# Expert gather with the down and the up row in one transfer, each row weighed by ScalarE as it comes

## The reference

```python
# q: 8 heads; two top-16 searches over 128 keys, and a top 16 over their 256 sums
eidx = ...                       # [T, 8 * 16]: 128 experts for each token
gate = softmax(top_s)            # [T, 8, 16]
def one(hh, ee, gg):             # 128 tokens at once
    a = einsum("tkd,td->tk", peer_down[ee], hh)   # 128 rows of 1024 for each token
    act = gg * gelu(a)
    return einsum("tk,tkd->td", act, peer_up[ee])
```

## Time and profile before

| | us |
|---|---|
| time, median of 3 runs (4175.64 to 4180.74) | 4179.28 |
| span of the profiled execution (the page gives no time outside it) | 4362.9 |
| TensorE busy | 3358.4 |
| VectorE busy | 2577.2 |
| ScalarE busy | 816.5 |
| GpSimd busy | 2040.9 |

### The profile page before, as it was taken

How to read it: one execution, slowest core, us unless ns; L and a number is a source line. 1 busy time by engine, 2 the same in 40 slices (tenths; PEclk the granted TensorE clock), 3 DMA queues, 4 the chain that set the end, 5 groups by cost and what they waited for, 6 DMA issues and landing times.

```text
span 4362.9 us, 35889 instructions
## 1 busy us (share of the span) xinstructions
PE 3358.4 (77%) x11238; PEld 1715.0 (39%) x11238; DVE 2577.2 (59%) x5454; ACT 816.5 (19%) x1926; POOL 2040.9 (47%) x2148
## 2 busy tenths in 40 slices
PE   6889686888767787887687766766878887866766
PEld 2357442356434243551354422221366654422111
DVE  1412768566686846676357674666563347684776
ACT  1311111321211122121211111111231211111111
POOL 0210566655555666666116665566000005676665
PEclk9999899999979899996899988866988998999556
DMA  6663998999999999999849999999400039999999
GB/s 228 227 237 130 338 363 320 375 356 409 401 362 355 343 378 352 392 410 375 298 159 369 333 365 392 372 405 374 157 1 1 1 113 338 352 350 372 379 369 346
DMA packets 380787, 1330.31 MB, mean 305 GB/s; under 512 B 39500, under 2 KB 44876, under 8 KB 377016
## 3 DMA queue, kind: packets, MB, share of 16 engines
q0 software_dynamic: 313344, 1141.10, 69.3%
q1 hardware_dynamic: 61104, 164.18, 10.1%
q10 hardware_dynamic: 6152, 22.74, 1.4%
HBM read 1326.69 MB, written 1.17 MB: 304 GB/s over the span
## 4 chain that ended last, share of the span: by engine, by line
PE 15%; DVE 10%; DMA 9%; issue 7%; POOL 5%; another core or an unknown queue 3%; ACT 2%; ACTq 0%; DVEq 0%; POOLq 0%
PE ps L1701 15%; POOL arena L3075 5%; DMA arena<-in_peer_up,arena 5%; DVE arena L893 3%; DVE arena L906 3%; DMA arena<-in_peer_v,arena 2%; ACT arena L2462 1%; DMA arena<-in_ada_w 1%; DMA arena<-in_peer_u,arena 1%; DMA arena<-in_peer_down,arena 1%; PE ps L1707 1%; DVE arena L914 1%; DVE arena L1287 1%; DVE arena L1282 0%
## 5 line engine op out<-in xcount | busy, mean ns | idle before, releaser
L1701 PE MATMUL ps<-arena 128*128 128x512 f32 (+9 forms) x10500 | 3254.6, 490 | 873.9 <-ACT arena L2462 231.9
L1701 PEld LDWEIGHTS ps<-arena 128*128 128x128 f32 (+4 forms) x10500 | 1621.6, 196 | 2435.2 <-issue 1844.2
L906 DVE SCALAR_TENSOR_TENSOR arena<-arena,ps 128x1024 f32<-128x1024 f32 x1024 | 1240.6, 1217 | 542.1 <-DMA arena<-in_peer_down,arena 289.1
L3075 POOL DMA_INDIRECT arena<-in_peer_down,arena x768 | 747.1, 973 | 654.8 <-DVE arena L910 269.5
L3075 POOL DMA_INDIRECT arena<-in_peer_up,arena x768 | 736.5, 959 | 541.2 <-PE ps L1701 294.3
L2462 ACT ACTIVATE arena<-arena 128x128 f32<-128x128 f32 (+5 forms) x1242 | 444.4, 387 | 1890.8 <-PE ps L1701 636.3
L3075 POOL DMA_INDIRECT arena<-in_peer_u,arena x256 | 248.4, 970 | 647.9 <-DVE arena L910 543.6
L906 DVE SCALAR_TENSOR_TENSOR ps<-arena,ps 128x512 f32<-128x512 f32 x508 | 383.4, 755 | 143.0 <-DMA arena<-in_peer_up,arena 88.8
L2462 ACT ACTIVATE arena<-ps 128x512 f32<-128x512 f32 (+4 forms) x349 | 191.5, 549 | 1165.6 <-PE ps L1701 547.9
L3075 POOL DMA_INDIRECT arena<-in_peer_v,arena x256 | 242.4, 947 | 149.2 <-issue 59.9
L893 DVE TENSOR_TENSOR arena<-arena 128x512 f32<-128x512 f32 (+8 forms) x398 | 246.9, 620 | 72.1 <-ACT arena L2462 42.1
(11 more groups left out here) (34 smaller groups left out, 565.1 us busy)
## 6 DMA issues: line engine op xcount, KB each, us to landing
arena<-in_w_mod POOLq DMA_DIRECT2D x40, 1024.0 KB, 6.6
arena<-in_gate_blocks SPq DMA_DIRECT2D x16, 2048.0 KB, 7.8
arena<-in_w_in SPq DMA_DIRECT2D x14, 2048.0 KB, 7.9
arena<-in_w_pq SPq DMA_DIRECT2D x13, 2048.0 KB, 16.0
arena<-in_ada_w POOLq DMA_DIRECT2D x24, 1024.0 KB, 8.3
arena<-in_w_out SPq DMA_DIRECT2D x8, 2048.0 KB, 8.0
arena<-in_gate_blocks SPq DMA_DIRECT2D x8, 1792.0 KB
arena<-mod_scratch ACTq DMA_DIRECT2D x26, 512.0 KB
```

The lines of the kernel that those rows point to most:

```text
L906: self.e.scalar_tensor_tensor(o, a, s, b, op0, op1, accum_out=accum).then_inc(*(inc or self.inc(self.S.vec)))
L1701: return self.e.matmul(o, l, r, start=start, stop=stop)
L3075: self.e.indirect_dma_start(out=o, out_offset=None, in_=table, in_offset=bass.IndirectOffsetOnAxis(ap=idx.bitcast(U32), axis=0)).then_inc( ...
```

## The change

- The host lays the down and the up row of an expert side by side in one table (`peer_rows`, `peer_rows_2`; a row of 2048 floats, 8 KB). One indirect DMA a step brings both into one of NR = 6 buffers of 8 KB a partition. GpSimd waits only until row s - 6 has been used up (`freed`).
- LAG becomes 1. ScalarE weighs each row at once (`weigh`): for the tanh form Square, Copy, Tanh and Identity on one column, for the exact form Gelu and Copy, then the diagonal as before. Each of these waits for the instruction before it. The constants of the tanh form are folded into the scale of the sum on VectorE and into the gates.
- The activation in groups of 16 and its multiplication on VectorE go. In odd tiles VectorE waits for the diagonal of row s - 1 before it adds its half.
- `fold` has three instructions instead of four and no buffer of its own. Some thresholds of `weave` are written relative to LAG, so that this work starts earlier by the 17 steps.
- The arena grows by 6 KB a partition and the scratch for descriptors shrinks from 8192 to 2048 bytes.

```diff
-ND = NU = 5
-GK = 16
-LAG = GK + 2
+NR = 6
+ASK = 16
+LAG = 1
...
+    def place(self, c):
+        return self.K.rows[c % NR], (self.S.row_in[c % NR], 16 * (c // NR + 1))
...
 # VectorE, gather
-                d, there = self.down_place(s)
+                buf, there = self.place(base + s)
                 self.wait_ge(*there)
-                self.stt(d, d, 1.0, K.HP, M, M, inc=self.inc(S.down), free=True, accum=K.AA[n % 2][:, k:k + 1])
-            if s >= GK + 1 and (s - 1) % GK == 0 and s - 1 <= total:
...
-                self.tt(w[:, ks], w[:, ks], K.GT[:, tiles[n_], ks], M, inc=self.inc(S.weighted), free=True)
+                d = buf[:, 0:D]
+                self.stt(d, d, GELU_Z if l < 2 else 1.0, K.HP, M, M, inc=self.inc(S.down), free=True, accum=K.AA[n % 2][:, k:k + 1])
...
+                    src, w = buf[:, D + 512:2 * D], K.AW[n % 2][:, k:k + 1]
+                    self.wait_ge(S.diagonal, c + 1)
...
 # TensorE, gather
-                buf, there = self.up_place(u, total)
+                buf, there = self.place(c)
...
 # ScalarE, gather
-                self.act(K.AW[n_ % 2][:, ks], K.AA[n_ % 2][:, ks], gelu, inc=self.inc(S.activated))
...
+                self.wait_ge(S.down, c + 1)
+                self.weigh(l, K.AA[n % 2][:, k:k + 1], K.GT[:, tiles[n], k:k + 1], K.AW[n % 2][:, k:k + 1], c % 2)
                 if c >= 4:
                     self.wait_ge(S.up_tensor, c - 3)
-                self.act(K.dg[c % 4], K.ident, ACT.Copy, scale=K.AW[n % 2][:, k:k + 1], inc=self.inc(S.diagonal), free=True)
+                self.act(K.dg[c % 4], K.ident, ACT.Copy, scale=K.AW[n % 2][:, k:k + 1], inc=self.inc(S.diagonal))
...
+    def weigh(self, l, a, gate, w, i):
+        cube, gated, curve = (self.K.curve[:, 3 * i + j:3 * i + j + 1] for j in range(3))
+        if l < 2:
+            self.act(cube, a, ACT.Square, scale=GELU_Q)
+            self.act(gated, a, ACT.Copy, scale=gate)
+            self.act(curve, cube, ACT.Tanh, scale=a, bias=a)
+            self.act(w, curve, ACT.Identity, scale=gated, bias=gated)
+        else:
+            self.act(curve, a, ACT.Gelu)
+            self.act(w, curve, ACT.Copy, scale=gate)
...
 # GpSimd, gather
-                if s >= ND:
-                    self.wait_ge(S.down, c - ND + 1)
...
-                o, there = self.down_place(s)
-                self.fetch(o, down, K.EI[:, tiles[n], k:k + 1], there[0])
...
-                self.fetch(o, up, K.EI[:, tiles[n], k:k + 1], there[0])
+                self.freed(max(0, s - NR + 1))
+                o, there = self.place(base + s)
+                self.fetch(o, table, K.EI[:, tiles[n], k:k + 1], there[0])
```

More of the change, by code:

```diff
@@ L147, in __init__ @@
         self.rows, self.units = 0, 0
-        self.base, self.shared, self.gathers = 0, 0, 0
+        self.base, self.shared = 0, 0
         self.halves_in = 0
@@ L485, in peer_topk, with gather @@
         yield from self.peer_pick(l, t, m, 0, 8)
-    def gather(self, tiles, tables, gelu, rows):
+    def gather(self, l, tiles, rows):
         total = NEXT * len(tiles)
@@ L717, in main @@
         done = self.until(queries, (0, 0))
-        self.weave(self.gather([0, 1, 2, 3], tables, gelu, [(0, 0, 5), (0, 0, 5), (0, 1, 5), (0, 1, 5)]),
+        self.weave(self.gather(0, [0, 1, 2, 3], [(0, 0, 5), (0, 0, 5), (0, 1, 5), (0, 1, 5)]),
                    ctx_then_x(queries), RATE0, done=done)
@@ L760, in queries_then_second @@
             self.second_mu()
-            yield ("after", NEXT + 5)
+            yield ("after", NEXT + LAG - 13)
             self.second_asked()
@@ L769, in queries_then_second @@
                 yield from self.z_block(0, j)
-        self.weave(self.gather([0, 1], tables, gelu, [(1, 0, 5), (1, 0, 5)]), queries_then_second(queries), RATE1, done=done)
+        self.weave(self.gather(1, [0, 1], [(1, 0, 5), (1, 0, 5)]), queries_then_second(queries), RATE1, done=done)
         self.folded(6)
@@ L1372, in gather @@
                 c = base + u
-                w = K.AW[n % 2][:, k:k + 1]
-                buf, there = self.up_place(u, total)
                 if n % 2:
[L1376 to L1389, removed]
+                    buf, _ = self.place(c)
+                    src, w = buf[:, D + 512:2 * D], K.AW[n % 2][:, k:k + 1]
+                    self.wait_ge(S.diagonal, c + 1)
+                    if self.halves(u):
+                        self.wait_ge(S.up_vector, self.halves(u))
+                    if k == 0:
+                        self.wait_ge(S.tile_done, c // NEXT)
+                        self.ts(K.av, src, w, None, M, None, inc=self.inc(S.up_vector), free=True)
+                    else:
+                        self.stt(K.av, src, w, K.av, M, AD, inc=self.inc(S.up_vector), free=True)
+                if k == NEXT - ASK:
                     gate = self.row()
@@ L2413, in steps @@
                         i.then_inc(*self.fill(made[d]))
-            self.place()
+            self.place_out()
             yield
@@ L2441, in steps, with place_out @@
         if bt == 3:
-            self.place()
-    def place(self):
+            self.place_out()
+    def place_out(self):
         K, S = self.K, self.S
@@ L3028, in modhalf, with gather @@
         yield from self.units_of(2)
-    def gather(self, tiles, tables, gelu, rows):
+    def gather(self, l, tiles, rows):
         K, S = self.K, self.S
         base, total = self.base, NEXT * len(tiles)
-        down, up = tables
+        table = K.A["peer_rows"] if l < 2 else K.A["peer_rows_2"]
         for s in range(total + LAG):
@@ L3258, in memory @@
     K.GR = GR = here()
[L3259 removed]
+    K.BG, K.GR2 = GR + 10 * D, GR + 4096
     K.wbuf += [arena[:, GR:GR + 4096], arena[:, KCR:KCR + 4096], arena[:, K.BG + 8320:K.BG + 12416]]
     K.sums = [K.wbuf[2][:, 0:2048], K.wbuf[2][:, 2048:4096], arena[:, NB:NB + 2048]]
[L3262 to L3266 removed]
+    gm = Mem(arena, (GR, K.BG), (NB, NB + 3 * D + 6))
+    K.rows = [gm(2 * D) for _ in range(NR)]
+    K.dg, K.AA, K.AW, K.curve = [gm(128) for _ in range(4)], [gm(128) for _ in range(2)], [gm(128) for _ in range(2)], gm(6)
     K.HP, K.ap, K.av = K.psum[:, 0:1024], K.psum[:, 1024:1536], K.psum[:, 1536:2048]
```

104 lines of the change are left out of this document (27 added, 77 removed).

## The result

The changed kernel takes **4312.5 us** (4306.3 to 4327.1, four runs) beside 4180.0 us (4175.6 to 4183.0) of the kernel before: ratio 1.0324, 95% interval 1.0304 to 1.0343. It is 132 us slower; 4030 was forecast, faster.

A forecast was written before the change was run, and what follows sets the result against it. Bound: gathers whose DMA engines, ceiling near 411 GB/s, run short because GpSimd is only 3% faster. Plain -64, edges -11, woven -80 make -155: 4363 to 4208, times 0.958 gives 4030 us; own range 3950 to 4120, 8 in 10 3900 to 4215.

The forecast's parts named there:

- so I scale all: Whole kernel: the profiled forecast of 4208 us was multiplied by 0.958, timed median over profiled span, giving 4030.
- plain term of -64: Gather stretches with little or no other work woven in: 723 us become 659 at 411 GB/s.
- GpSimd, transfers: Gathers: one indirect DMA fewer a step, 1270 us less; transfers stay at 411 GB/s, 3% either way.
- stays under 2.55 a step: ScalarE gains some 1060 us of work, an estimated 1.85 us a step, yet fits the 2.55 us DMA step.
- landing term: Row buffers: a row takes 6.6 us to land, part of the 12.2 us that its buffer is held.
- slack of 3.1 us: Row buffers: six allow 15.3 us at 2.55 a step, against 12.2 us that a row is held.
- Woven stretches, -80: Gather stretches with other work woven in: faster transfers save 80 us, bounds -231 and +168.
- bound of +168: Woven stretches, slow side: a 20.5 us loop over six buffers makes 678 steps of 3.42 us, +168 us.
- I take half: Woven stretches: of about 165 us gain, half was taken, as sum, weighing and TensorE now follow one another.
- Six buffers are too few: Rival, woven stretches: copies waiting for TensorE delay weighing and buffer release, so GpSimd stops; 4269 us, chance 0.20.
- Tables: Rival, ScalarE: Tanh shares no function set with woven Exp and Sigmoid, up to 192 us of loads; 4215, chance 0.04.
- the edges, -11: Starts and ends of the gathers: 332.9 us become 322 at 411 GB/s plus landings and tails, -11 us.

The follow-up runs named there:

- a_free: The changed kernel with constant weights, so the weighing is left out and ScalarE waits for no sum; 4120.0 us.
- b_again: The kernel before, unchanged, profiled again because its first profiled execution (span 4362.9 us) was odd; 4179.1 us, profiled span 4175.9.
- b_load: The kernel before with four chained activations on a constant column ahead of every diagonal, results unused; 4295.7 us.
- a_five: The changed kernel with five buffers of 8 KB instead of six; 4407.2 us.
- a_lag3: The changed kernel with TensorE and VectorE's second half three rows behind the sum instead of one; 4416.3 us.
- a_free5: The changed kernel with constant weights, the weighing left out, and five buffers in place of six; 4205.1 us.
- v_gelu2: The changed kernel two rows behind, layers 0 and 1 weighed by two activations (Gelu's tanh form, then the gate) in place of four; 4224.1 us.

## Why the prediction was wrong

Two steps failed. The first is the slack read from the odd execution: a_free, which has all of the change but the weighing, took 4120, so 90 of the 282 us between the forecast 4030 and 4312 are gains that aren't there even without it. The second is the woven stretches: the weighing's order there was named as a cost and got no price of its own, only half of a gain; the runs put it at 193 us, 79 for ScalarE's bare work and 114 for waiting for the sum.

**The time of before, "so I scale all": wrong.** The three gathers of the odd execution took 3205.9 us; in b_again they take 1563 + 767 + 692 = 3022 (447 to 2010, 2188 to 2955, from 3484), and the rest 1154 beside 1157. All of the excess lay in the gathers; it was the very slack that I meant to win. Half of it was slower packets and not idle DMA: q0's packets took 69.3% of 4362.9 us, 3023, and in b_again 70.1% of 4175.9, 2927, for the same bytes. The earlier trace rows had a sign of it: from a share of 1.03 to 0.95 the engines' work falls by 8%, and the rate by 17%. I read it as too little work for them. The plain term of -64 rests on 2.86 us a step; ordinary is 2.59, and 253 x 0.05 = 13 us is what it is worth. "GpSimd is only 3% faster than the DMA engines", and so the queue runs dry: the pace is right (0.94 + 0.30 us in b_again too), but in b_again DMA is full in two of the three woven pieces nonetheless (shares 1.01 and 1.02 above). The span 4.4% over the median was on the first page; the stretch to suspect was the one that the argument needed.

**GpSimd, transfers: right.** 0.96 us an issue, half of them; 419 against 411 GB/s, inside the 3%.

**ScalarE: sizes right, conclusion wrong.** 1.85 us were worked out, 1.86 ran (above); 1060 us more work, and the column's form grew by 1117.0 - 13.8 = 1103; table loads 48:

```profile
L2441 ACT ACTIVATE arena<-arena 128x1 f32<-128x1 f32 x3652 | 1117.0, 306 | 1016.3 <-DVE arena L898 837.0 <-DVE arena L893 31.7 <-DVE arena L885 21.2
L2441 ACT ACTIVATE arena<-arena 128x128 f32<-128x128 f32 x1038 | 415.3, 400 | 97.1 <-ACT arena L2441 1.5 <-PE ps L1681 1.4
...
L2441 ACT ACT_TABLE_LOAD x48 | 61.6, 1283 | 51.7 <-DVE arena L885 29.8 <-PE ps L1681 12.5 <-issue 3.8
```
But "stays under 2.55 a step" holds for a plain step only, where it cost nothing (419 GB/s). In a woven step ScalarE's queue also has copies out of PSUM, and b_load shows 114 us for the work alone.

**Buffers: right for plain rows, wrong where it mattered.** The landing term was 6.6 us, from a direct transfer of 1 MB; the joined rows land in 9.1, and rows of half the size in 9.1 to 9.6 in b_again. But the landing is no fixed term: it is 7.7 us with five buffers (a_five) and 10.3 in a_free. So putting 9.1 into the sum, a loop of 14.7, isn't the mending: by it a plain step with five buffers would take 2.94 us, and a_five's takes 2.58 (65 in 168 us, above), a loop of at most 12.9 beside the 12.2 worked out. The estimate from the Trainium skill ("DMA: Bandwidth & Descriptors", section "Anatomy of one DMA — SWDGE (gpsimd) path"), 4.4 us, lies further off than 6.6. The slack of 3.1 us was a slack of plain steps (a_lag3, which holds a row two steps longer, uses it up). In woven ones there was none: a_five and a_free5 lose 85 to 95 us for one buffer.

**Woven stretches, -80: wrong in sign.** After is 136 us longer while the plain rows won some 13: about +150 in woven stretches and edges, near the bound of +168. "I take half" set a gain against a cost that I named (sum, weighing and TensorE one behind the other) and left without a price of its own. Most of the gain wasn't there: at 411 GB/s the three gathers of b_again, which move 388 to 393, would be some 160 us shorter, those of the odd execution 350, and a_free got 60 in all. (The 165 isn't 95 scaled by length either: 95 x 2150 / 1433 is 143.)

**The rivals.** *Six buffers are too few* (4269) came nearest, but its place was half right: woven copies that wait for TensorE ahead of the weighing aren't most of it; ScalarE now waits 840 us for sums and 790 for TensorE (2086 in b_again). The chain through VectorE's and TensorE's woven work and ScalarE's own load hold the row. Its loop of 19.0 us was passed: 119 us for 32 rows is 3.72 a step, 22 for six. *Tables* fell: 48 loads, fewer than 81. The Trainium skill's list of sets ("ScalarE: Activation LUTs", section "Table sets: the hidden batching unit"), with tanh beside exp and beside sigmoid, agrees with that.

**Open.** More than six buffers weren't run. What made packets slower and DMA idler in the one execution of before isn't known, nor what the edges, -11, came to.

## What to carry to other kernels

Before a slack is spent, see that the profiled execution is as long as the timed runs, and if not, in which stretch the excess lies. Joining two transfers makes the second half occupy its buffer while the first is still being worked on; test the depth with one buffer fewer before relying on it (here 85 to 95 us for 8 KB), and look in the woven rows, since the plain ones hardly noticed. An engine that is 44% busy in the mean still costs when its new work stands in order between others that wait for each other: price it by adding the bare work to the kernel before.

## What the runs showed of the hardware that was not expected

A joined row of 8 KB moved at 419 GB/s where two of 4 KB moved at 409 (plain pieces above), for 147,000 packets fewer: 2%, no more. How long such a row takes to land isn't fixed: 7.7 us with five buffers, 9.1 with six, 10.3 with six and no weighing. Weighing row by row with the tanh form of Gelu loaded tables 196 times in v_gelu2, with Square, Tanh and Identity 48 times, 1.28 us each: of the 40 to 57 us that two activations fewer were to give (half of 79 or 114), 21 were left.
